# A seventh slot in the weight stream from the linear attention on, with the first half's bias rows, modulation sums, columns and vectors lying in it

## What is computed

```python
def first_block(x, c, ...):
    cond = silu(c)
    for l in range(2):
        mod = cond @ w_ada[l] + b_ada[l]          # six vectors of 1024: shifts, scales, gains
        h = layer_norm(x) * (1 + sc1) + sh1
        x = layer_norm(a * x + g1 * mixer(h), ln1_g[l], ln1_b[l])
        h = layer_norm(x) * (1 + sc2) + sh2
        x = layer_norm(a * x + g2 * moe(h), ln2_g[l], ln2_b[l])   # 16 experts, inner width 256
...
def second_block(x, ...):
    h = x
    for layer in range(2):
        mix = gla_mixer(h) if layer == 0 else diff_attention(h, k1, k2, v)
        h = layer_norm(a * h + mix, ...)
        h = layer_norm(a * h + hier_moe(h), ...)                  # 16 experts, inner width 512
        if layer == 0: k1, k2, v = shared_kv(h)
    return h
```

## Time and profile before

| | |
|---|---|
| median of 3 runs | 1626.11 us (1622.19, 1626.11, 1626.22) |
| the profiled execution | 1622.02 us |
| its span, first to last instruction | 1620.2 us |
| TensorE matmuls, busy | 1503.9 us |
| VectorE, ScalarE, GpSimd busy | 549.3, 339.6, 132.8 us |
| bytes moved by DMA | 462.65 MB, of which the stream 212 slots |
| mean granted TensorE clock | 0.969 |

### The profile page before, as it was taken

One profiled execution on the slowest core, in us unless ns is written; L12 is line 12 of the kernel. 1 busy time (PEld: TensorE's weight loads), 2 busy tenths in 40 slices (PEclk: granted clock), 3 DMA queues, 4 the chain that ended last, 5 costly groups with the idle time before them and its releaser, 6 DMA issues.

```text
span 1620.2 us, 16716 instructions
## 1 busy us (share of the span) xinstructions
PE 1503.9 (93%) x7088; PEld 849.2 (52%) x7088; DVE 549.3 (34%) x1022; ACT 339.6 (21%) x735; POOL 132.8 (8%) x73
## 2 busy tenths in 40 slices
PE   5999999999799999989989998999888998999985
PEld 2777874454367787445436444434335764443332
DVE  2682345421555235542141034121104354221113
ACT  3113231321211313132132123111102243111101
POOL 0005630000000820000000000000002000000000
PEclk9999999799799999989999998999999999999998
DMA  9985344799456731579936425999998433899995
GB/s 382 396 318 214 145 167 182 307 387 414 193 229 248 271 149 60 196 313 391 413 166 217 173 104 214 428 427 429 427 427 332 156 125 150 336 429 426 427 427 223
DMA packets 34565, 462.65 MB, mean 286 GB/s; under 512 B 4432, under 2 KB 4560, under 8 KB 6160
## 3 DMA queue, kind: packets, MB, share of 16 engines
q1 hardware_dynamic: 31376, 447.34, 67.6%
q0 software_dynamic: 3104, 14.12, 2.7%
HBM read 458.29 MB, written 3.15 MB: 285 GB/s over the span
## 4 chain that ended last, share of the span: by engine, by line
PE 78%; DMA 15%; DVE 5%; ACT 1%; issue 1%; SPq 0%; DVEq 0%; ACTq 0%
PE work L743 15%; PE work L561 12%; DMA ring<-in_stream 9%; PE work L544 7%; PE work L796 7%; PE acc L561 7%; DMA area<-in_stream 6%; PE acc L544 5%; PE work L700 4%; PE work L553 3%; PE acc L778 2%; PE work L1223 2%; PE acc L1368 2%; PE work L1026 1%; PE work L761 1%
## 5 line engine op out<-in xcount | busy, mean ns | idle before, releaser
L743 PE MATMUL work<-ring,area 128*64 128x512 f32 x832 | 186.3, 595 | 11.7 <-DMA ring<-in_stream 11.6
L561 PE MATMUL work<-ht_sb,ring 128*128 128x256 f32 x576 | 132.1, 390 | 1.0 <-DMA ring<-in_stream 1.0
L743 PEld LDWEIGHTS work<-ring,area 128*64 128x64 f32 x832 | 58.4, 137 | 131.0 <-issue 108.3
L561 PEld LDWEIGHTS work<-ht_sb,ring 128*128 128x128 f32 x576 | 111.9, 196 | 21.2 <-issue 4.2
L2352 DVE SCALAR_TENSOR_TENSOR area<-area,comb_slot,work 128x256 f32<-128x256 f32 (+1 forms) x32 | 19.6, 614 | 300.3 <-ACT area L1591 300.3
L561 PE MATMUL acc<-ht_sb,ring 128*128 128x256 f32 x512 | 114.1, 382 | 0.0
L743 PE MATMUL work<-area 128*64 128x512 f32 x448 | 101.0, 594 | 7.2 <-DMA area<-in_stream 7.1
L561 PEld LDWEIGHTS acc<-ht_sb,ring 128*128 128x128 f32 x512 | 96.3, 190 | 15.9 <-issue 3.3
L2364 DVE TENSOR_TENSOR area_r<-work,area_r 128x512 fp32r<-128x512 f32 x64 | 44.3, 692 | 170.2 <-ACT area_r L1599 137.7
L1591 ACT ACTIVATE area<-work 128x256 f32<-128x256 f32 (+1 forms) x32 | 15.7, 491 | 343.6 <-PE work L743 343.6
L796 PE MATMUL work<-area 128*64 128x512 f32 x384 | 87.7, 599 | 0.0
(11 more groups left out here) (326 smaller groups left out, 1926.5 us busy)
## 6 DMA issues: line engine op xcount, KB each, us to landing
ring<-in_stream SPq DMA_DIRECT2D x133, 2048.0 KB, 12.2
area<-in_stream SPq DMA_DIRECT2D x60, 2048.0 KB, 12.2
cst<-in_stream SPq DMA_DIRECT2D x19, 2048.0 KB, 16.7
ln_sb<-in_ln_vecs POOLq DMA_DIRECT2D x8, 1024.0 KB, 12.0
rel_rows<-mt_sb POOLq DMA_DIRECT2D x1, 2048.0 KB, 50.4
cst<-in_consts POOLq DMA_DIRECT2D x1, 1465.5 KB, 13.2
x_sb<-in_x SPq DMA_DIRECT2D x1, 1024.0 KB, 16.5
area<-rel_rows POOLq DMA_DIRECT2D x8, 128.0 KB, 2.8
```

The source lines that it names most:

```text
L561: ins = pe.matmul(dst, w[:, k, c0:c0 + n], src[:, k0 + k, :], start=k == 0, stop=k == ks - 1)
L743: ins = pe.matmul(banks[half][e * CAP:(e + 1) * CAP, :], tokens[:, k, at:at + CAP], w[:, kk, e, half * W:(half + 1) * W], start=k == 0, st ...
```

## The change

An eighth bank, number 7 of the numbering above, is the new tile `early` (128 x 4096 floats). It is open from gla_out to the end. Until then it holds `row`, `ada_acc`, the first 392 columns (`col_early`: c, router, mix norms, b_ada) and the first 528 short vectors (`vec_early`). SyncE issues the first load into it, gla_out's first half, after `k_decayed`. To let the early parts lie together, columns and vectors are put in another order; `col` and `vec` keep the rest. So the columns are loaded in two pieces and `N_FIRST` is 3; the vectors are loaded in two pieces as well. `silu_wide` lies in the unused last 512 columns of the constants, which are no longer loaded. `SQ2` lies in `area`. The number of banks open in the experts of the second half is seven instead of six, of which one still opens at the fifth slot. The first half has the banks it had.

```diff
@@ OPEN
-        RING + 3: ((0, SLOTS["ada0_0"]),)}
+        RING + 3: ((0, SLOTS["ada0_0"]),),
+        RING + 4: ((SLOTS["gla_out"], N_SLOTS),)}
@@ build
-        cst, vec, col = sb("cst", N_CONST + 2 * D), sb("vec", N_VECS), sb("col", N_COLS)
+        cst, vec, col = sb("cst", N_CONST + 2 * D), sb("vec", N_VECS - N_EARLY_VECS), sb("col", N_COLS - N_EARLY_COLS)
...
-        row = sb("row", N_ROWS, 32)
-        ada_acc = sb("ada_acc", 2 * W)
+        early = sb("early", SLOT)
+        row, ada_acc = early[0:32, 0:N_ROWS], early[:, N_ROWS:N_ROWS + 2 * W]
+        col_early = early[:, N_ROWS + 2 * W:N_ROWS + 2 * W + N_EARLY_COLS]
+        vec_early = early[:, N_ROWS + 2 * W + N_EARLY_COLS:N_ROWS + 2 * W + N_EARLY_COLS + N_EARLY_VECS]
+        silu_wide = cst[:, CONST["spare"][0]:CONST["spare"][0] + KD * 32]
...
-        silu_wide = sb("silu_wide", KD * 32)
...
         ring.append(area[:, 1792:1792 + SLOT])
+        ring.append(early[:, :])
...
-            return col[:, o:o + n].rearrange("p (a b) -> p a b", a=a)
+            return col_at(o, n).rearrange("p (a b) -> p a b", a=a)
...
-        SQ2 = ada_acc[:, 0:W].rearrange("p (t e d) -> p t e d", t=TT, e=2)
+        SQ2 = area[:, 13312:13312 + W].rearrange("p (t e d) -> p t e d", t=TT, e=2)
...
-        N_FIRST, N_INPUTS = 2, 1
+        N_FIRST, N_INPUTS = 3, 1
@@ block.sync
-            sp.dma_start(col[:, :], cols).then_inc(first_loaded, 16)
+            sp.dma_start(col_early, cols[:, 0:N_EARLY_COLS]).then_inc(first_loaded, 16)
             sp.dma_start(cst[:, 0:N_EARLY], consts[:, 0:N_EARLY]).then_inc(first_loaded, 16)
+            sp.dma_start(col[:, :], cols[:, N_EARLY_COLS:N_COLS]).then_inc(first_loaded, 16)
             sp.dma_start(slot(0)[:, :], stream[0, :, :]).then_inc(slot_loaded[RING_BANK[0]], 16)
...
                 if first_of_span(s) and b == RING + 2:
                     sp.wait_ge(rel_row_ready, 1)
+                elif first_of_span(s) and b == RING + 4:
+                    sp.wait_ge(k_decayed, 1)
@@ block.gpsimd
-            pool.dma_start(vec[:, :], bass.AP(vecs.tensor, 0, [[0, P], [1, N_VECS]])).then_inc(tables_loaded, 16)
-            pool.dma_start(cst[:, N_EARLY:N_CONST], consts[:, N_EARLY:N_CONST]).then_inc(tables_loaded, 16)
+            pool.dma_start(vec_early, bass.AP(vecs.tensor, 0, [[0, P], [1, N_EARLY_VECS]])).then_inc(tables_loaded, 16)
+            pool.dma_start(vec[:, :], bass.AP(vecs.tensor, N_EARLY_VECS, [[0, P], [1, N_VECS - N_EARLY_VECS]]))\
+                .then_inc(tables_loaded, 16)
+            pool.dma_start(cst[:, N_EARLY:CONST["spare"][0]], consts[:, N_EARLY:CONST["spare"][0]]).then_inc(tables_loaded, 16)
```

More of the change, by code:

```diff
@@ L97 @@
 N_VECS = 0
-for _name, _n in (("qn0", HD), ("qn1", HD), ("kn0", HD), ("kn1", HD), ("router_bias", NE), ("b_group0", 4),
-                  ("b_router0", NE), ("b_group1", 4), ("b_router1", NE),
-                  ("lq1", HD), ("lk1", HD), ("lq2", HD), ("lk2", HD)):
+for _name, _n in (("qn0", HD), ("qn1", HD), ("kn0", HD), ("kn1", HD), ("router_bias", NE),
+                  ("lq1", HD), ("lk1", HD), ("lq2", HD), ("lk2", HD), ("b_group0", 4),
+                  ("b_router0", NE), ("b_group1", 4), ("b_router1", NE)):
     VECS[_name] = (N_VECS, _n)
     N_VECS += _n
+N_EARLY_VECS = VECS["b_group0"][0]
 COLS = {}
 N_COLS = 0
-for _name, _n in (("c", KD), ("router", KD * 32), ("route0", KD * 32), ("route1", KD * 32), ("lr", KD * LR), ("g_sub", 1), ("g_norm", KD),
-                  *((f"norm{i}", 2 * KD) for i in range(4)), *((f"mix{l}", 2 * KD) for l in range(DEPTH)), *((f"b_ada{l}", 6 * KD) for l in range(DEPTH))):
+for _name, _n in (("c", KD), ("router", KD * 32), *((f"mix{l}", 2 * KD) for l in range(DEPTH)),
+                  *((f"b_ada{l}", 6 * KD) for l in range(DEPTH)), ("route0", KD * 32), ("route1", KD * 32), ("lr", KD * LR), ("g_sub", 1), ("g_norm", KD),
+                  *((f"norm{i}", 2 * KD) for i in range(4))):
     COLS[_name] = (N_COLS, _n)
     N_COLS += _n
+N_EARLY_COLS = COLS["route0"][0]
 ROWS = {}
@@ L280, in vector_, with col_at @@
             o, n = VECS[name]
-            return vec[:, o:o + n]
+            return vec_early[:, o:o + n] if o < N_EARLY_VECS else vec[:, o - N_EARLY_VECS:o - N_EARLY_VECS + n]
+        def col_at(o, n):
+            return col_early[:, o:o + n] if o < N_EARLY_COLS else col[:, o - N_EARLY_COLS:o - N_EARLY_COLS + n]
         def column(name, a=KD):
             o, n = COLS[name]
-            return col[:, o:o + n].rearrange("p (a b) -> p a b", a=a)
+            return col_at(o, n).rearrange("p (a b) -> p a b", a=a)
         def norm_columns(i, name="norm"):
             o, _ = COLS[f"{name}{i}"]
-            return col[:, o:o + KD], col[:, o + KD:o + 2 * KD]
+            return col_at(o, KD), col_at(o + KD, KD)
         def rows_(name, parts):
@@ L1456, in _ @@
             act.wait_ge(first_loaded, 16 * N_FIRST)
[L1457 removed]
+            act.activation(silu_c[:, :], col_at(0, KD), ACT.Silu).then_inc(act_chain, 1)
             C.made(act_chain)
             act.wait_ge(consts_set, 2)
[L1460 removed]
+            act.activation(silu_wide[:, :].rearrange("p (k n) -> p k n", k=KD)[:, :, 0], col_at(0, KD), ACT.Silu)\
                .then_inc(silu_spread, 1)
@@ L1667, in ada_out @@
                     ins = act.activation(mod_col[:, o + c:o + c + 1], bank[:, c:c + 1], ACT.Identity,
-                                         bias=col[:, b + 4 * n + c:b + 4 * n + c + 1])
+                                         bias=col_at(b + 4 * n + c, 1))
                     if c == 0:
@@ L2912 @@
         [a["c"].reshape(KD, P).T, blocked(to_32(a["w_router"]))]
+        + [a[n][l].reshape(KD, P).T for l in range(DEPTH) for n in ("ln1_g", "ln1_b")]
+        + [a["b_ada"][l].reshape(6 * KD, P).T for l in range(DEPTH)]
         + [blocked(to_32(np.concatenate([a["moe_w_group_2"][l], a["moe_w_router_2"][l]], 1))) for l in range(DEPTH)]
@@ L2916 @@
         + [v.reshape(KD, P).T for v in (a["ln2_g"][1], a["ln2_b"][1], *(
-            a[n][l][i] for l, i in ((0, 0), (0, 1), (1, 0)) for n in ("ln_g_2", "ln_b_2")),
-                                          *(a[n][l] for l in range(DEPTH) for n in ("ln1_g", "ln1_b")))]
-        + [a["b_ada"][l].reshape(6 * KD, P).T for l in range(DEPTH)], 1)
+            a[n][l][i] for l, i in ((0, 0), (0, 1), (1, 0)) for n in ("ln_g_2", "ln_b_2")))], 1)
     rows = np.zeros((32, N_ROWS), a["b_ada"].dtype)
```

14 lines of the change are left out of this document (6 added, 8 removed).

## The result

The changed kernel takes 1613.45 us (median of 5 runs, 1612.05 to 1616.53), the kernel before beside it 1626.22 us (1622.19 to 1627.74): a ratio of 0.993, 95% interval 0.9914 to 0.9947. By the ratio that is 11.4 us less, from 8.6 to 14.0. The profiled execution of the changed kernel is its median, 1613.45 us with a span of 1611.6; that is 8.6 us less span than the profile of before. The prediction said 1616.6, between 1610.5 and 1620.0, and 9.5 us less, profile to profile.

The account below looks back on a forecast made before the run. DMA's pace in moe2 and moe3 was taken as the bound. Terms -4.9 - 4.9 + 0.3 = -9.5 us gave 1612.5 from the profiled 1622.02 us, or 1616.6 against the median 4.1 us above it; range 1610.5 to 1620.0.

Parts of the forecast that it names:

- The bound, and what a slot buys: In moe2 and moe3 DMA sets the pace; a seventh slot gives one transfer's head start, 4.9 us gained in each.
- The walk over the ring: Before moe2, loads 112 to 114 issue together at about 986, the last landing at 1003.7; the same holds in moe3.
- (d): SQ2, silu_wide, bias rows and first columns at other addresses, same shapes and instruction count: cost 0.
- (a): SyncE waits for k_decayed before gla_out's first half; the load goes 5.1 us later, at cost 0.
- (b): At the start, three loads instead of two stand ahead of the stream: cost 0.3 us, between 0 and 0.8.
- (c): One more GpSimd load for vectors in two pieces, and 256 KB fewer constants: cost 0, no gain.
- (e): In the attention after moe2, the relative bias lands behind one more stream slot: cost 0, at worst 1.7 us.
- (f): At stage borders the clock may meet a moved border otherwise: taken as 0, with 3 us kept both ways.
- Hidden latency: Rival: the 25.6 us turn is latency that more loads in flight hide, giving 1603.3 us; chance 0.02.
- One head start lost: Rival: moe2's extra load lands late, or late bias or code before moe3 eats the gain, 1621.5 us; chance 0.06.
- Hidden anyway: Rival: the load is hidden anyway or no load is added ahead of the experts, 1626.4 us; chance 0.03.
- the slower stream: Rival: with seven loads queued and one in the early data's tile, the stream moves less, 1634 us; chance 0.02.

Follow-up runs that it names:

- the halves: Changed kernel with the seventh slot open only from gla_out to moe2's end (1617.3 us, ratio 0.9946), or only from v on (1618.48 us, ratio 0.995).
- the same layout: Changed kernel with its new layout and three column loads, but the seventh slot never opened: 1622.47 us, ratio 0.9979.
- The late slot: Changed kernel with the seventh slot opened only from the thirteenth slot of moe2 and of moe3: 1622.76 us, ratio 0.9982.
- the split-column run: Kernel before with its first load, the columns, issued as two loads and nothing else changed: 1626.71 us, ratio 1.0005.
- the megabyte taken out of a stage: Changed kernel with GpSimd's 1 MB norm-vector loads in moe2 and moe3 waiting until the stage's last slot has landed: 1608.42 us, ratio 0.99.
- the two that hold the stream back: Changed kernel with slots behind moe2 issued only after its last slot is used: alone 1610.33 us, with late norm-vector loads too 1607.71 us.

## Why the prediction was right, point by point

**The bound, and what a slot buys.** Right, and this is the step that the runs test hardest. The pace is the DMA's (428 GB/s with five, six and seven slots), and a seventh slot is worth one transfer at the start of each stage: 5.2 and 4.0 us for the halves, 9.0 us for both against the same layout (8.0 by the ratios), 9.8 predicted; in the stages themselves 4.6 and 4.8 us, where 4.9 each was predicted. The late slot separates this from its look-alike, more loads in flight: turns of 30.41 us, no gain.

**The walk over the ring.** Right: slots 112 to 114 were issued at 986.36, 986.73 and 987.20, predicted "together at about 986", and the last landed at 1004.54, predicted 1003.7. In moe3 slot 170 landed at 1382.00, 2.6 us before the first release at 1384.64. The turn was forecast at 30.5 us and is 30.41; the idle time left at 6.7 us a stage and is 7.2 and 7.0. One of my signs of being wrong did show: moe2 from first release to last landing shrank by 5.4 us and not 4.9. The part that the head start gives is 4.6; 0.8 is the layout's, under (d).

**(a)** k_decayed: right. Slot 106 was issued at 883.72, 5.9 us later than before, of which 5.1 was worked out, and nothing waited for it.

**(b)** The start: +0.3 was wrong in sign. The stream's slot 0 landed at 10.72, 0.9 us earlier than before, and TensorE got its weights earlier too:

```profile
1.66 0.42 SPq L441 DMA_DIRECT2D col<-in_cols  x1
...
23.11 0.20 PEld L914 LDWEIGHTS acc<-ring,cst 128*32 128x32 f32 x8 [4.63 <-DMA ring<-in_stream]
```

That is at 23.11 in place of 24.01, after a longer wait but an earlier one. Yet the time at which slot 4 was released moved from 51.75 to 52.55, and the kernel before alone moves it from 51.75 to 53.42 between its two profiles. Nor is the 0.9 firm: slot 0 lands at 11.85 in the repetition of the kernel before, and between 10.62 and 12.33 in the kernels of the new layout. Neither the predicted 0.3 nor the 0.9 reaches the end measurably; the split-column run says so with a ratio of 1.0005.

**(c)** and the reading speed in (d): right, 593 to 594 ns a matmul from the tile early.

**(d)** Other addresses at a cost of nothing: this is the term that was wrong. I asked what an engine pays to read at another address and not what the DMA pays to write there. It was worth 0.8 us a stage, and 3.4 us (1.5 to 5.4) on the whole kernel. The two stages hold 1.6 of it, which the interval allows to be all; whether the earlier stages hold the rest isn't shown. The landings tie it to the loads' addresses: 0.018 us a slot, all of it in the two slots of `area`, is 0.8 us over the 42 slots of a stage.

**(e)** The relative bias: no cost, as predicted, with 5.87 us to spare where 3.2 were worked out.

```profile
1236.77 8.46 POOL L533 DMA_DIRECT2D area<-rel_rows  x16
1250.29 4.71 DVE L2681 TENSOR_TENSOR area<-area,cst 128x384 f32<-128x384 f32 x8 [14.34 <-DMA area<-rel_rows]
1260.87 1.02 DVE L2689 SCALAR_TENSOR_TENSOR area<-acc,area 128x384 f32<-128x384 f32 x2 [5.87 <-PE acc L1332]
```

I held the bias at its old time and moved the scores by 4.9 us. The bias came 1.16 us earlier (1250.29 against 1251.45), and the scores 3.41 (1260.87 against 1264.28): 8.12 + 1.16 - 3.41 = 5.87. But GpSimd had issued its 16 loads 4.07 us earlier (1236.77 against 1240.84). So they took longer: the last one 5.5 us from issue to landing in place of 2.6, beside a backlog of the stream that ended at 1245.7 in place of 1243.4, where I had held it at the same time. The rule of the Trainium skill on turns between queues ("DMA: Bandwidth & Descriptors", Queues, rings and completion order) would have made the bias wait longer by up to one slot; the trace agrees, with 2.9 us more, inside that one slot, and the earlier issue covered it.

**(f)** The clock: 0, with 3 us either way, held. In the profiles the gain at moe2's end was 4.6 us and fell to 3.1 by moe3's first release (167.62 us between the two, against 166.14). ScalarE's pause has 0.5 of that (4.91 against 4.40 us), and the clock, at 0.69 for 0.80, goes with the rest. The kernel before with its columns split lost more at the same place (168.75 us).

**The rivals.** Hidden latency (1603.3) fell with the late slot. One head start lost (1621.5) fell with the two halves. Hidden anyway (1626.4) and the slower stream (1634) fell with the ratio and with 425 GB/s. The rule of the Trainium skill ("DMA: Bandwidth & Descriptors", Specifications), about 358 GB/s for a core, would have a slot at an estimated 5.9 us; by that rule the megabyte taken out of a stage gives an estimated 2.9 us. Measured were 2.45 us, and 4.88 for a slot. That its 1614.7 is nearer to the measured 1613.45 than the forecast is luck.

**The sum.** The term for the layout, put at 0, measured -3.4 us, and the start 0 in place of +0.3. The head starts, forecast at -9.8, are -9.4 in the two stages and -8.0 in the whole kernel by the ratios; the difference is within the intervals. So the measured -11.4 (-8.6 to -14.0) is -8.0 and -3.4. The number 1616.6 came out 3.2 us high, and two things that the prediction didn't know stand behind that. One is the layout. The other is the profile of before, which was 4.1 us under its median: the prediction carried that gap over to the changed kernel, where the profile and the median are the same. That the range still held, with a term of 3.4 us for which it had left no room, is in part luck.

## What to carry to other kernels

A deeper ring in front of a stage that the DMA bounds bought one transfer's time, once per stage, with the slot full when the stage began. The engine must have that much idle time to give, and here it had 11.5 us. Opened at the thirteenth slot it bought nothing here, though the queue was longer. So before adding a slot, look at what else moves in the saturated window: a megabyte of loads that no one needs yet cost half a slot's gain in each stage here and took two lines a stage to move. And where a change shifts addresses, give the transfers a line of their own in the sum, measured with the layout alone.

## What the hardware showed that was not expected

The rate of one and the same stream depends a little on where in SBUF it lands: 4.892 to 4.899 us for 2,097 KB in the three profiles with the old addresses, 4.875 to 4.888 with the changed kernel's (the rows of the table above), 4.858 to 4.862 in the one profile with nearly all of them moved. The rule behind it is open.

ScalarE's pause before the table load at moe2's end is 4.4 to 5.1 us in the twelve profiles with the stream's backlog running, and 2.2 and 2.9 us in the two that hold the stream back; at moe3's end, with no slot behind, it is 1.8 to 2.1 us in all of them. The chain gives it to no semaphore. It stands in the chain of every kernel here but the two that hold the stream back, where the late slot stands in its place.
